# Moving a filter network's DMA issues from ScalarE's queue to SyncE's, and its steps closer together

## The chip, the cores and the metric

The kernel runs on one core of one Trainium2 chip. The metric is the device time of one execution in microseconds (us), from start to end of the program. It is one launch, with all layers inside.

## What is computed

The reference is a small hybrid network over 512 positions and 1024 features. It begins with two layers, each a mixer followed by a convolutional feed-forward block, and goes on with a second network of two layers (attention with a latent, then a Hyena mixer). Two pieces matter here. The first feed-forward block, `ffn(0)`:

```python
gate, val = jnp.split(x @ w_up, 2, axis=-1)        # 1024 -> 2 x 2816
conv = conv_b + sum(conv_w[j] * shifted(gate, j))  # width 3, along positions
y = (jax.nn.silu(conv) * val) @ w_down             # 2816 -> 1024
```

And two computations that don't depend on it, whose work is woven between its matmuls: the modulation rows of the later layers (`silu(c) @ ada_w`, called ada below), and the filters of the Hyena mixer. The latter come from a network over positions: three matmuls of 64 x 64, each followed by a sine (the hidden steps), then an output matmul whose rows are multiplied by a decay, folded into sums and differences, and kept in device memory until the Hyena mixer reads them.

## The kernel before

**Weights.** All weight matrices pass as one stream of chunks, each of 8 tiles of 128 x 128. SyncE loads a chunk (512 KB) into one of 4 `raw` buffers; ScalarE rounds it to a high half `whi` (L1195), VectorE subtracts to a low half `wlo` (L1871), with 3 buffers of each. TensorE does three matmuls a tile: high by high (L324), high by low (L327), low by high (L328). SyncE may load chunk c once the low half of chunk c - 4 is made; ScalarE may split chunk c once TensorE has begun chunk c - 2.

**`ffn(0)`** has two halves. Each half is an up pass of 11 rounds f (gate projection of 8 tiles, value projection of 8 tiles: two chunks a round), and a down pass of 8 projections i of 11 tiles. The first half takes chunks 40 to 72, the second 73 to 105. After each round VectorE and ScalarE run `tail(f)`: eviction of the gate (gp), convolution (c0, c1, c2), tanh, eviction of the value (v), products (s2, mo), high half (hh) and low half (hl) of the result. `tail` also contains two column products of ada (L2086, L2089), the first right behind gp and the second behind mo; behind that one is the filter's step.

**The filter's steps** are generators, one in each engine's program, advanced by `next(rows)`: once in each round f from 1 on, and in the down passes behind tile 9 of each projection and behind tile 4 of some. TensorE steps after a round's gate projection, ScalarE and VectorE in its `tail`. The generators must have the same number of steps. A unit n (four of them) has: wr (weights summed and subtracted, L2160), w_hi and w_lo (their halves, L1384, L2165), then eight steps ht (n, i, x) of two matmuls (L573, L574), which VectorE multiplies by the decay into `ab` (L2174). GpSimd (`folded`) adds and subtracts the two x of an i into `sd` (L2729).

**Their DMAs** are issued by ScalarE, in its own generator: the unit's weights (`weights`, L1353 and L1354), the decay (`decay`, L1359, for each x once at the unit's start and once for its second half), and the storing of `sd` to device memory (`keep`, L1364). Each issue waits in ScalarE's program order for its producer.

**SyncE's order** is written out by marks. TensorE's program, while it is built, notes at a place how many chunks it has begun, plus 3; SyncE issues the weights up to that chunk and then what the mark names. So far the marks in this block name the 24 ada rows of 512 KB (L2802, into 3 buffers), one for a round or projection, noted behind its last tile:

```python
def mark(self, name, more=0):
    self.s.marks[name] = -(-len(self.spec) // 8) + 3 + more
...
for name, at in sorted(s.marks.items(), key=lambda x: x[1]):
    weights(done, at)
    done = max(done, at)
```

Of the kernel before, what the change touches and what calls it, by code (L numbers as in the profile page):

```python
# [17 lines left out]
KD = 8  # L18
# [262 lines left out]
MLA_BANKS = [{"tr0": 7, "tr1": 4, "qn": 5, "kn": 7, "knc": 4, "sg": 5}, {"qn": 7, "kn": 4, "knc": 5, "sg": 7}]  # L281
MLA_OUT_BANKS = [7, 4, 5, 3, 0, 1, 2, 6]
ROWS_AT = [(5, 2), (5, 6), (6, 2), (6, 6), (7, 0)]
two_steps = lambda half, i: i % 2 or half == 0 and i > 3
UNITS = [(0, 0), (1, 0), (0, 1), (1, 1)]


# [27 lines left out]
def tensor_program(e, m, s):  # L315
# [230 lines left out]
    def filter_rows():  # L546


        a = m.ffn[0]
        for l in range(3):  # L550
            if l:
                q.wait_ge(*s.made_a.at("hdn", l - 1))
            else:
                q.wait_ge(*s.pos.at())
                q.wait_ge(*s.filt.at())
                q.wait_ge(*s.rb.at("n1"))
            src = a.fa[:, 1, :] if l else a.pos[:, :]
            e.matmul(B[7][0:64, :], a.fw[:, l, :], src, start=True, stop=True).then_inc(*s.filled.tick("hid", l))
            yield
            yield  # L560
        for n in range(4):
            yield
            yield
            for i in range(4):
                for x in range(2):
                    if x or i or n:
                        q.wait_ge(*s.taken_v.at("ht", *((n, i, 0) if x else (n, i - 1, 1) if i else (n - 1, 3, 1))))
                    else:
                        q.wait_ge(*s.made_v.at("fx", 2))
                    q.wait_ge(*s.made_v.at("w_lo", n, i % 2))  # L570
                    q.wait_ge(*s.made_v.at("hdl", 1))
                    cs = slice(256 * x + 128 * (i // 2), 256 * x + 128 * (i // 2) + 128)
                    e.matmul(B[7], a.hd[:, cs], a.ws[:, i % 2, :], start=True, stop=False)  # L573
                    e.matmul(B[7], a.hdl[:, cs], a.ws[:, i % 2, :], start=False,  # L574
                             stop=True).then_inc(*s.filled.tick("ht", n, i, x))
                    yield
        yield

    def ffn(layer):
# [34 lines left out]
        for half in range(2):  # L614
            for f in range(half * HF, half * HF + HF):
                run(project(2 * f % 6, up, f, ("gate", layer, f), nhi, nlo, bank_free(half, f, 0),
                            ready0 if f == 0 else nothing, then=behind(f, 0)))
                if f:
                    another()
                run(project((2 * f + 1) % 6, up, FT + f, ("val", layer, f), nhi, nlo, bank_free(half, f, 1),  # L620
                            then=behind(f, 1)))
                if f > 1:
                    next(ad, None)

            def ready(k, half=half):
                q.wait_ge(*s.hid_lo.at("f", layer, half * HF + k))

            for i in range(KD):
                f0 = half * HF + HF - 3

                def free(i=i, f0=f0):
                    if i >= 6:
                        q.wait_ge(*s.h.at(dn, half, i - 6))
                        return
                    for f in range(f0, f0 + 3):
                        for j in range(2):
                            if (2 * f + j) % 6 == i:
                                q.wait_ge(*s.taken_v.at("gv"[j], layer, f))
                run(project(i % 6, dn, i, (dn, half, i), hh, hl, free, ready, ks=HF, k0=half * HF,
                            then={4: another, 9: another} if two_steps(half, i) else {9: another}))  # L640
                if half == 0:
                    next(ad, None)

# [539 lines left out]
            yield  # L1183


def scalar_program(e, m, s, A, chunks):
    q = Waits(e)
    pc = Views(m).par
    B, PS, stat, par = m.bank, m.PS, m.stat, m.par
# [155 lines left out]

    def filter_rows():
        a = m.ffn[0]

        def weights(n):
            od, c = UNITS[n]  # L1350
            base = od * 2048 + 512 * c
            q.wait_ge(*(s.taken_v.at("ht", n - 1, 3, 1) if n else s.hid_lo.at("o", KD - 1)))
            e.dma_start(a.wd[64:128, 0, :], A["filt_out"][:, base:base + 512]).then_inc(*s.fo0.tick(n))  # L1353
            e.dma_start(a.wd[64:128, 1, :], A["filt_out"][:, base + 1024:base + 1536]).then_inc(*s.fo1.tick(n))  # L1354

        def decay(n, k, x):
            c = UNITS[n][1]
            q.wait_ge(*(s.taken_v.at("ht", n, 1, x) if k else s.made_v.at("w_lo", n, 1)))
            e.dma_start(a.wd[:, x, :], A["decay"][:, 2 * x + k, 512 * c:512 * c + 512]).then_inc(*s.dc[x].tick(n, k))  # L1359

        def keep(n, i):
            for x in range(2):
                q.wait_ge(*s.made_p.at("sd", n, i, x))
                e.dma_start(A["rows"][UNITS[n]][:, 4 * (i % 2) + 2 * x + i // 2, :],  # L1364
                            a.sd[:, x, :]).then_inc(*s.kept[x].tick(n, i))

        for l in range(3):
            q.wait_ge(*s.made_v.at("fa", l))
            e.activation(a.fa[:, 1, :], a.fa[:, 0, :], ACT.Sin).then_inc(*s.made_a.tick("hdn", l))
            if l == 2:  # L1370
                q.wait_ge(*s.made_a.at("hdn", 2))
                for x in range(2):
                    e.activation(a.hd[64 * x:64 * x + 64, :], a.fa[:, 1, :], ACT.Copy).then_inc(*s.made_a.tick("hd", x))
            yield
            if l == 1:
                weights(0)
            yield
        for n in range(4):
            if n:
                keep(n - 1, 3)  # L1380
            q.wait_ge(*(s.filled.at("ht", n - 1, 3, 1) if n else s.filled.at("hid", 2)))
            for j in range(2):
                q.wait_ge(*s.made_v.at("wr", n, j))
                e.activation(a.ws[0:64, j, :], a.wd[0:64, j, :], ACT.Copy).then_inc(*s.made_a.tick("w_hi", n, j))  # L1384
            yield
            for x in range(2):
                decay(n, 0, x)
            yield
            for i in range(4):
                for x in range(2):  # L1390
                    if i and x == 0:
                        keep(n, i - 1)
                    if i == 1:
                        decay(n, 1, x)
                    elif i == 3 and x and n < 3:
                        weights(n + 1)
                    yield
        keep(3, 3)
        yield

    def ffn(layer):
        a = m.ffn[layer]
# [21 lines left out]
        for half in range(2):  # L1424
# [19 lines left out]
            for i in range(KD):  # L1444
                for k in range(HF):
                    w.tiles(1)
                    if k == 9 or k == 4 and two_steps(half, i):
                        next(rows, None)
                if half and layer == 0:
                    after("n2", "attn_norm", i, (dn, 1), free=("val", 0, FT - 1))  # L1450
                elif half:
                    q.wait_ge(*s.h.at(dn, 1, i))
                    if i > 1:
                        q.wait_ge(*s.made_v.at("n4f", i - 1))
                        q.wait_ge(*s.acc.at("n4", i - 1))
                    e.activation(m.sqb[:, 1, :] if i else m.rb2[:, :], m.hT[:, i, :], ACT.Square,
                                 scale=m.fg[:, i:i + 1]).then_inc(*s.sq.tick("n4f", i))
                    e.activation(m.sqb[:, 0, :] if i else m.acc, m.hT[:, i, :], ACT.Square,
                                 scale=D ** -0.5).then_inc(*s.sq.tick("n4", i))
# [404 lines left out]
def vector_program(e, m, s, chunks):  # L1864
# [280 lines left out]
    def filter_rows():  # L2145
        a = m.ffn[0]
        for l in range(3):
            hidden(l)
            yield
            yield  # L2150
        for n in range(4):
            if n == 0:
                for x in range(2):
# [23 lines left out]
    def ffn(layer):  # L2177
# [37 lines left out]
        for half in range(2):  # L2215
# [14 lines left out]
            for i in range(KD):  # L2230
                for k in range(HF):
                    w.tiles(1)
                    if k == 9 or k == 4 and two_steps(half, i):
                        next(rows, None)
                if half == 0:
                    next(ad, None)
# [445 lines left out]
def pool_program(e, m, s):  # L2682
# [57 lines left out]
            folded(n, i)  # L2740
    for i in range(1, KD):
        sum_of_squares("n2", i)
        if i in (2, 3, 4, 6):
            folded(3, (2, 3, 4, 6).index(i))
    q.wait_ge(*s.filled.at("down0", 1, KD - 1))
    e.memset(m.swa.kz[:, :, :, :], 0.0).then_inc(*s.made_p.tick("kz"))
    e.memset(m.swa.vz[:, :, :, :, :], 0.0).then_inc(*s.made_p.tick("vz"))
# [33 lines left out]
def sync_program(e, m, s, A, chunks):  # L2781
# [11 lines left out]
    def ada_rows(layer, n):  # L2793
# [2 lines left out]
            q.wait_ge(*s.made_v.at("col", layer, 1 - layer, n - r))  # L2796
        elif layer == 0:
            q.wait_ge(*s.hid_lo.at("o", KD - 1))
        else:
            for x in range(2):  # L2800
                q.wait_ge(*s.kept[x].at(3, 3))
        e.dma_start(m.ffn[layer].aw[:, n % r, :], A["ada"][layer, n]).then_inc(*s.ada_w[n % r].tick(layer, n))  # L2802

    def filter_rows(od, c, j):
        if od or c:
# [17 lines left out]
    for name, at in sorted(s.marks.items(), key=lambda x: x[1]):  # L2823
# [13 lines left out]
            e.dma_start(m.ffn[0].fw[:, :, :], A["filt"]).then_inc(*s.filt.tick())  # L2837
        elif name[0] == "ada":
            ada_rows(*name[1:])
        else:  # L2840
            filter_rows(*name[1:])
    weights(done, NONE)
# [6 lines left out]
def build(nc, A, chunks, counted, notes):  # L2849
# [3 lines left out]
    with ExitStack() as ctx:  # L2853
# [24 lines left out]

        @block.scalar
        def _(e):  # L2880
            passed.append(scalar_program(e, m, s, A, chunks))

        @block.vector
        def _(e):
# [193 lines left out]
```

## Time and profile before

| | |
|---|---|
| median of 3 runs | 2054.27 us (2053.4 to 2057.48) |
| profiled execution, its own time | 2053.4 us |
| its span, first to last instruction | 2051.6 us |
| TensorE matmul busy | 1981.9 us, 97% |
| VectorE busy | 1381.3 us, 67% |
| ScalarE busy | 828.3 us, 40% |
| GpSimd busy | 231.9 us, 11% |
| mean granted TensorE clock | 0.987 of full speed |
| DMA | 208.4 MB, mean 102 GB/s |

PE is TensorE's matmul, PEld its weight load, DVE VectorE, ACT ScalarE, POOL GpSimd, SP SyncE; a q behind an engine is its sequencer, which waits and issues. L324 is line 324. The engines run at the same time, so busy shares don't add up to the span; what sets the time is which engine the others wait for at each place.

### The profile page before, as it was taken

Reading aid. Unit: us, or ns where it says so; the run is one execution under the profiler, and the core shown is the slowest. Engines: PE = TensorE matmul, PEld = TensorE weight load, DVE = VectorE, ACT = ScalarE, POOL = GpSimd, SP = SyncE. Lnnn points to the kernel's source line nnn. Section 1 sums busy time; section 2 is a strip of 40 time slices with the busy share of each in tenths; the row PEclk is TensorE's granted clock in tenths of the full one; section 3 lists DMA queues with packets and bytes.
Section 4 is the critical chain, followed back from the end, with each engine's and each line's share of the span. In section 5 each row is a group of like instructions: output and inputs, shape, how many; then the busy total and the mean of one; then the engine's idle time right before and its main releaser. Section 6 shows DMA issues by size and latency. Waiting matters only on the chain.

```text
span 2051.6 us, 24676 instructions
## 1 busy us (share of the span) xinstructions
PE 1981.9 (97%) x9878; PEld 1655.7 (81%) x9878; DVE 1381.3 (67%) x1961; ACT 828.3 (40%) x1259; POOL 231.9 (11%) x234
## 2 busy tenths in 40 slices
PE   8999999999999999999999999999999999999987
PEld 6888887778878888888888888778888878888776
DVE  5577765887789667756764784555555567787774
ACT  5333324442233345544432443444334444454442
POOL 2133221002201230010000001100000101001011
PEclk9999999999999999999999999999999999999998
DMA  5211113335534340123344333311111323232321
GB/s 190 63 64 53 52 56 99 124 133 180 192 138 163 123 144 32 42 62 140 140 161 134 125 132 103 103 62 42 42 42 32 115 81 117 96 137 91 126 83 51
DMA packets 60963, 208.40 MB, mean 102 GB/s; under 512 B 6832, under 2 KB 7152, under 8 KB 59696
## 3 DMA queue, kind: packets, MB, share of 16 engines
q1 hardware_dynamic: 53296, 193.19, 27.9%
q10 hardware_dynamic: 7552, 13.64, 1.9%
q8 instruction: 78, 1.28, 0.3%
q14 instruction: 37, 0.30, 0.0%
HBM read 196.31 MB, written 10.49 MB: 101 GB/s over the span
## 4 chain that ended last, share of the span: by engine, by line
PE 75%; DVE 16%; ACT 5%; issue 3%; DMA 0%; POOL 0%; ACTq 0%; SPq 0%; DVEq 0%
PE PS L324 19%; PE PS L328 19%; PE PS L327 19%; DVE wlo L1871 3%; PE PS L436 2%; PE PS L935 2%; DVE col_f L2086 2%; ACT whi L1195 1%; PE PS L331 1%; PE PS L334 1%; PE PS L335 1%; PE PS L924 1%; PE PS L687 1%; PE PS L386 1%; PE PS L728 1%
## 5 line engine op out<-in xcount | busy, mean ns | idle before, releaser
L324 PE MATMUL PS<-nhi,whi 128*128 128x512 f32 x1456 | 594.0, 408 | 20.9 <-DVE wlo L1871 5.9
L328 PE MATMUL PS<-nhi,wlo 128*128 128x512 f32 x1456 | 572.3, 393 | 0.0
L327 PE MATMUL PS<-nlo,whi 128*128 128x512 f32 x1456 | 571.1, 392 | 0.0
L1871 DVE TENSOR_TENSOR wlo<-raw,whi 128x1024 fp32r<-128x1024 f32 x291 | 368.7, 1276 | 183.0 <-ACT whi L1195 181.9
L1195 ACT ACTIVATE whi<-raw 128x1024 fp32r<-128x1024 f32 x291 | 303.1, 1052 | 211.7 <-PE PS L324 143.9
L324 PEld LDWEIGHTS PS<-nhi,whi 128*128 128x128 f32 x1456 | 276.4, 190 | 84.1 <-issue 11.3
L328 PEld LDWEIGHTS PS<-nhi,wlo 128*128 128x128 f32 x1456 | 275.6, 189 | 60.1
L327 PEld LDWEIGHTS PS<-nlo,whi 128*128 128x128 f32 x1456 | 276.8, 190 | 53.6 <-issue 2.6
L2713 POOL TENSOR_TENSOR diag<-diag,sqb 128x512 f32<-128x512 f32 (+1 forms) x56 | 73.1, 1305 | 783.9 <-ACT sqb L1204 701.3
L324 PE MATMUL PS<-hh_f,whi 128*128 128x512 f32 x352 | 137.2, 390 | 0.0
L328 PE MATMUL PS<-hh_f,wlo 128*128 128x512 f32 x352 | 137.0, 389 | 0.0
L327 PE MATMUL PS<-hl_f,whi 128*128 128x512 f32 x352 | 136.9, 389 | 0.0
L2729 POOL TENSOR_TENSOR sd_f<-ab_f 128x512 f32<-128x512 f32 x32 | 54.4, 1717 | 280.1 <-DVE ab_f L2174 279.5
L2086 DVE SCALAR_TENSOR_TENSOR col_f<-aw_f,scv,col_f 128x1024 f32<-128x1024 f32 x63 | 85.0, 1358 | 0.0
L328 PEld LDWEIGHTS PS<-hh_f,wlo 128*128 128x128 f32 x352 | 66.1, 188 | 13.8
L324 PEld LDWEIGHTS PS<-hh_f,whi 128*128 128x128 f32 x352 | 66.1, 188 | 13.7
L327 PEld LDWEIGHTS PS<-hl_f,whi 128*128 128x128 f32 x352 | 66.1, 188 | 13.7
L1413 ACT ACTIVATE t_f<-gp_f,par 128x512 f32<-128x512 f32 x44 | 35.9, 817 | 90.4 <-DVE gp_f L2191 90.4
L1659 ACT ACTIVATE pt_m<-PS 128x768 f32<-128x768 f32 x32 | 25.9, 811 | 111.8 <-PE PS L924 111.8
L1915 DVE TENSOR_TENSOR hT<-hT,PS 128x512 f32<-128x512 f32 x48 | 32.7, 682 | 52.2 <-PE PS L328 52.2
L436 PEld LDWEIGHTS PS<-qa,kk 128*128 128x128 f32 x448 | 56.0, 191 | 14.2 <-DVE qa L2023 10.3
L1204 ACT ACTIVATE sqb<-hT 128x512 f32<-128x512 f32 x42 | 26.5, 630 | 99.1 <-DVE hT L1915 62.4
(356 smaller groups left out, 3374.9 us busy)
## 6 DMA issues: line engine op xcount, KB each, us to landing
raw<-in_stream SPq DMA_DIRECT2D x291, 512.0 KB, 3.5
aw_f<-in_ada SPq DMA_DIRECT2D x48, 512.0 KB, 4.5
rows<-sd_f ACTq DMA_DIRECT2D x32, 256.0 KB, 2.2
rows_h<-rows SPq DMA_DIRECT2D x8, 1024.0 KB, 6.2
wd_f<-in_decay ACTq DMA_DIRECT2D x16, 256.0 KB, 3.0
hT<-in_xT SPq DMA_DIRECT2D x8, 256.0 KB, 6.8
out<-hT SPq DMA_DIRECT2D x8, 256.0 KB, 2.0
wd_f<-in_filt_out ACTq DMA_DIRECT2D x8, 128.0 KB, 2.8
```

Of the source, the lines that this page charges most:

```text
L324: op = e.matmul(out, hi, xh, start=first, stop=False)
L327: e.matmul(out, hi, xl, start=False, stop=False)
L328: return e.matmul(out, lo, xh, start=False, stop=last)
L436: op = e.matmul(B[b][:, cs], kk[:, z, cs], qx[:, cs], start=True, stop=True)
L935: op = e.matmul(B[6][:, 128 * blk:128 * blk + 128], a.v[:, t, 128 * h:128 * h + 128], a.pt[:, i, 128 * t:128 * t + 128], start=t == 0, sto ...
L1195: e.activation(m.whi[:, c % HL, :], m.raw[:, c % RAW, :], ACT.Copy).then_inc(*s.w_hi.tick(c))
L1413: e.activation(a.t[:, 0, z, :], a.gp[:, z, 2:T + 2], ACT.Identity, bias=pc(cb, f), scale=pc(cw, 44 + f)).then_inc(*s.made_a.tick("c0", lay ...
L1871: e.tensor_tensor(m.wlo[:, c % HL, :], m.raw[:, c % RAW, :], m.whi[:, c % HL, :].bitcast(F), SUB).then_inc(*s.w_lo.tick(c))
L1915: op = e.tensor_tensor(h, h, B[b], ADD)
L2086: e.scalar_tensor_tensor(col[:, v, :], aw[:, n % AW[layer], :], m.scv[:, 2, k, v:v + 1], col[:, v, :], MUL, ADD).then_inc(*s.made_v.tick(" ...
L2713: e.tensor_tensor(acc, acc, m.sqb[:, i % 2 if site != "n4" else 0, 0:width], ADD).then_inc(*s.acc.tick(site, i))
L2729: e.tensor_tensor(a.sd[:, x, :], a.ab[:, 0, :], a.ab[:, 1, :], SUB if x else ADD).then_inc(*s.made_p.tick("sd", n, i, x))
```

## The change

The DMA issues of the filter rows are taken out of ScalarE's generator. TensorE's generator notes marks for them, and SyncE issues them in the order of the marks, with the same waits. At equal places the mark noted first comes first.

The generators lose three steps: a hidden step is followed at once by the next (before, an empty step stood behind each). So the hidden steps stand at rounds 1, 2 and 3, where they stood at 1, 3 and 5, and every later step comes three steps earlier. The down pass of the first half has two steps for the odd projections only (before, also for 4 and 6). GpSimd's last four folds stand at other places among its sums of squares. And the first ada load of layer 1 no longer waits for the last stores.

```diff
-two_steps = lambda half, i: i % 2 or half == 0 and i > 3
...
@@ tensor_program, filter_rows
             else:
+                tiles.mark(("filter", 0))
                 q.wait_ge(*s.pos.at())
...
             e.matmul(B[7][0:64, :], a.fw[:, l, :], src, start=True, stop=True).then_inc(*s.filled.tick("hid", l))
             yield
-            yield
         for n in range(4):
-            yield
-            yield
+            if n:
+                tiles.mark(("kept", n - 1, 3))
+                tiles.mark(("filter", n))
+            yield
+            yield
+            for x in range(2):
+                tiles.mark(("decay", n, 0, x))
             for i in range(4):
                 for x in range(2):
+                    if i and x == 0:
+                        tiles.mark(("kept", n, i - 1))
+                    if (i, x) in ((1, 1), (2, 0)):
+                        tiles.mark(("decay", n, 1, 1 - x))
...
+        tiles.mark(("kept", 3, 3))
         yield
...
@@ tensor_program, ffn (the same in scalar_program and vector_program)
-                            then={4: another, 9: another} if two_steps(half, i) else {9: another}))
+                            then={4: another, 9: another} if i % 2 else {9: another}))
...
@@ scalar_program, filter_rows
-        def weights(n):
-        def decay(n, k, x):
-        def keep(n, i):
...
-            if l == 1:
-                weights(0)
-            yield
         for n in range(4):
-            if n:
-                keep(n - 1, 3)
...
-            yield
-            for x in range(2):
-                decay(n, 0, x)
-            yield
-            for i in range(4):
-                for x in range(2):
-                    if i and x == 0:
-                        keep(n, i - 1)
-                    if i == 1:
-                        decay(n, 1, x)
-                    elif i == 3 and x and n < 3:
-                        weights(n + 1)
-                    yield
-        keep(3, 3)
-        yield
+            for _ in range(10):
+                yield
...
@@ vector_program, filter_rows
         for l in range(3):
             hidden(l)
             yield
-            yield
...
@@ pool_program
-        if i in (2, 3, 4, 6):
-            folded(3, (2, 3, 4, 6).index(i))
+        if i in (1, 2, 4, 5):
+            folded(3, (1, 2, 4, 5).index(i))
...
@@ sync_program
-        else:
-            for x in range(2):
-                q.wait_ge(*s.kept[x].at(3, 3))
         e.dma_start(m.ffn[layer].aw[:, n % r, :], A["ada"][layer, n]).then_inc(*s.ada_w[n % r].tick(layer, n))
+
+    def filter_weights(n):
+        od, c = UNITS[n]
+        base = od * 2048 + 512 * c
+        wd = m.ffn[0].wd
+        q.wait_ge(*(s.taken_v.at("ht", n - 1, 3, 1) if n else s.hid_lo.at("o", KD - 1)))
+        e.dma_start(wd[64:128, 0, :], A["filt_out"][:, base:base + 512]).then_inc(*s.fo0.tick(n))
+        e.dma_start(wd[64:128, 1, :], A["filt_out"][:, base + 1024:base + 1536]).then_inc(*s.fo1.tick(n))
+
+    def decay(n, k, x):
+        c = UNITS[n][1]
+        q.wait_ge(*(s.taken_v.at("ht", n, 1, x) if k else s.made_v.at("w_lo", n, 1)))
+        e.dma_start(m.ffn[0].wd[:, x, :], A["decay"][:, 2 * x + k, 512 * c:512 * c + 512]).then_inc(*s.dc[x].tick(n, k))
+
+    def keep(n, i):
+        for x in range(2):
+            q.wait_ge(*s.made_p.at("sd", n, i, x))
+            e.dma_start(A["rows"][UNITS[n]][:, 4 * (i % 2) + 2 * x + i // 2, :],
+                        m.ffn[0].sd[:, x, :]).then_inc(*s.kept[x].tick(n, i))
...
+        elif name[0] == "filter":
+            filter_weights(*name[1:])
+        elif name[0] == "decay":
+            decay(*name[1:])
+        elif name[0] == "kept":
+            keep(*name[1:])
```

## Rows read from the trace of the kernel before

**Rows 1.** The page: the chain that ended last, by engine.

```profile
PE 75%; DVE 16%; ACT 5%; issue 3%; DMA 0%; POOL 0%; ACTq 0%; SPq 0%; DVEq 0%
```

**Rows 2.** Windows of the passes: busy PE, PEld, DVE, ACT, POOL; granted clock, DMA share, GB/s.

```profile
345.00:475.00 130.00, 123.99 (x536) 98.28 (x536) 109.66 (x142) 57.42 (x70) 0.00 (x0) 0.99 0.39 133
475.00:542.00 67.00, 66.33 (x296) 54.68 (x296) 51.64 (x50) 12.98 (x14) 23.86 (x16) 1.00 0.56 199
542.00:665.00 123.00, 121.05 (x537) 99.71 (x535) 101.37 (x118) 41.44 (x51) 15.16 (x10) 0.97 0.44 153
665.00:760.00 95.00, 95.00 (x428) 78.67 (x428) 59.70 (x72) 37.21 (x51) 32.98 (x23) 0.98 0.40 128
```

**Rows 3.** Waits of TensorE, 350 to 760 us: total us, times, longest us.

```profile
PE PS L324 <- DVE wlo L1871: 3.2, 2, 2.8
PE PS L573 <- DVE ws_f L2165: 3.0, 2, 2.1
PE PS L573 <- DVE ab_f L2174: 2.3, 4, 0.7
```

**Rows 4.** Timeline of TensorE: start, us, line, tiles [idle before <-releaser].

```profile
355.11 1.07 PE L558 MATMUL PS<-pos,fw 64*64 64x512 f32 x2
...
361.70 0.39 PE L324 MATMUL PS<-nhi,whi 128*128 128x512 f32 x1
...
367.14 0.39 PE L324 MATMUL PS<-nhi,whi 128*128 128x512 f32 x1
...
402.24 1.07 PE L558 MATMUL PS<-fa,fw 64*64 64x512 f32 x2
...
422.65 0.80 PE L324 MATMUL PS<-nhi,whi 128*128 128x512 f32 x1 [2.78 <-DVE wlo L1871]
...
453.77 0.47 PE L573 MATMUL PS<-ws_f,hd_f 128*128 128x512 f32 x1 [2.07 <-DVE ws_f L2165]
...
454.31 0.40 PE L324 MATMUL PS<-nhi,whi 128*128 128x512 f32 x1
```

**Rows 5.** Timeline of VectorE, first up pass.

```profile
423.65 0.68 DVE L2191 TENSOR_TENSOR gp_f<-PS,rb 128x512 f32<-128x512 f32 x1
...
433.07 0.68 DVE L2191 TENSOR_TENSOR gp_f<-PS,rb 128x512 f32<-128x512 f32 x1
...
439.63 1.40 DVE L2155 TENSOR_TENSOR hdl_f<-fa,hd_f 64x512 fp32r<-64x512 f32 x2
441.06 1.29 DVE L2160 TENSOR_TENSOR wd_f<-wd_f 64x512 f32<-64x512 f32 x2
...
459.37 1.27 DVE L2086 SCALAR_TENSOR_TENSOR col_f<-aw_f,scv,col_f 128x1024 f32<-128x1024 f32 x1
```

**Rows 6.** Waits of all engines, 450 to 755 us.

```profile
ACT whi L1195 <- DVE ab_f L2174: 25.0, 5, 10.3
...
ACT whi L1195 <- POOL sd_f L2729: 20.4, 3, 10.3
```

**Rows 7.** Timelines of VectorE and ScalarE, hidden step 0.

```profile
365.87 0.80 DVE L2126 TENSOR_SCALAR fa<-PS,par 64x512 f32<-64x512 f32 x1
...
369.95 0.63 ACT L1369 ACTIVATE fa<-fa 64x512 f32<-64x512 f32 x1 [2.04 <-DVE fa L2142]
```

**Rows 8.** Tiles sd_f, rows and aw_f: durations in ns and us to landing, min/median/max.

```profile
L2729 POOL TENSOR_TENSOR sd_f<-ab_f x32: 1279/1591/2287, 475.2 to 744.2; 128x512 f32<-128x512 f32 x32
...
L1364 ACTq DMA_DIRECT2D rows<-sd_f x32: 321/332/445, 476.6 to 745.6; - x32
...
DMA to landing us min/median/max: 4.2/4.5/6.7
```

**Rows 9.** Timeline of SyncE's queue.

```profile
445.25 0.33 SPq L2788 DMA_DIRECT2D raw<-in_stream  x1
445.62 0.43 SPq L2802 DMA_DIRECT2D aw_f<-in_ada  x1
```

**Rows 10.** Tile hh_f: first and last start of the down-projection's matmuls.

```profile
L324 PE MATMUL PS<-hh_f,whi x352: 389/389/486, 475.6 to 1295.9; 128*128 128x512 f32 x176
```

More of the change, by code:

```diff
@@ L1183, in steps, with scalar_program @@
             yield
-def scalar_program(e, m, s, A, chunks):
+def scalar_program(e, m, s, chunks):
     q = Waits(e)
@@ L1347, in filter_rows @@
         a = m.ffn[0]
-        def weights(n):
[L1350 to L1354, printed above, removed]
-        def decay(n, k, x):
-            c = UNITS[n][1]
-            q.wait_ge(*(s.taken_v.at("ht", n, 1, x) if k else s.made_v.at("w_lo", n, 1)))
-            e.dma_start(a.wd[:, x, :], A["decay"][:, 2 * x + k, 512 * c:512 * c + 512]).then_inc(*s.dc[x].tick(n, k))
-        def keep(n, i):
-            for x in range(2):
-                q.wait_ge(*s.made_p.at("sd", n, i, x))
-                e.dma_start(A["rows"][UNITS[n]][:, 4 * (i % 2) + 2 * x + i // 2, :],
-                            a.sd[:, x, :]).then_inc(*s.kept[x].tick(n, i))
         for l in range(3):
@@ L1446, in ffn @@
                     w.tiles(1)
-                    if k == 9 or k == 4 and two_steps(half, i):
+                    if k == 9 or k == 4 and i % 2:
                         next(rows, None)
@@ L2232, in ffn @@
                     w.tiles(1)
-                    if k == 9 or k == 4 and two_steps(half, i):
+                    if k == 9 or k == 4 and i % 2:
                         next(rows, None)
@@ L2798, in ada_rows @@
             q.wait_ge(*s.hid_lo.at("o", KD - 1))
-        else:
-            for x in range(2):
-                q.wait_ge(*s.kept[x].at(3, 3))
         e.dma_start(m.ffn[layer].aw[:, n % r, :], A["ada"][layer, n]).then_inc(*s.ada_w[n % r].tick(layer, n))
+    def filter_weights(n):
[14 more added lines that the diff above has]
+                        m.ffn[0].sd[:, x, :]).then_inc(*s.kept[x].tick(n, i))
     def filter_rows(od, c, j):
@@ L2880, in _ @@
         def _(e):
-            passed.append(scalar_program(e, m, s, A, chunks))
+            passed.append(scalar_program(e, m, s, chunks))
         @block.vector
```

## The prediction, made before the change was run

> **What bounds the kernel now.** The reading starts with the chain of work that ended last: three quarters of it is TensorE [rows 1], so only what makes TensorE wait, repeat work or run slow can move the time. The change touches only the first feed-forward block, which lies between 345 and 760 us, so the windows come next [rows 2]. They cut that stretch into its four passes: first up-projection, first down-projection, second up, second down. TensorE is idle for 6.0, 0.7, 1.95 and 0 us in them, 8.6 us of 415. The waits view names whom it waited for [rows 3]: 8.5 us in all, always VectorE, either for the low half of a weight chunk or for the filter rows. The granted clock of the first, third and fourth windows is 0.99, 0.97 and 0.98, which is 1.3, 3.7 and 1.9 us lost at the lower level (1.2 instead of 2.4 GHz).
>
> The block's own beat is read from two starts. A chunk of 8 weight tiles (24 matmuls) takes 367.14 - 361.70 = 5.44 us [rows 4]. One round f of an up pass is two chunks, 10.9 us on TensorE, and a filter-row matmul pair adds 0.54 us (454.31 - 453.77). VectorE's round, from one gate eviction to the next, is 433.07 - 423.65 = 9.4 us without any filter work [rows 5]; a filter step adds 0.7 (an ht product, as gp), 1.3 (w_lo, two operations like wr) or 2.7 us (hdl 1.40 and wr 1.29). So in the up passes VectorE has about 1 us a round to spare. That is the number on which this case turns: whatever delays VectorE there is handed to TensorE nearly in full.
>
> **The change, part by part.**
>
> *Issues leave ScalarE.* 56 DMA issues (32 kept, 16 decay, 8 filter weights) of 0.32 to 0.6 us each [rows 8] are some 20 us of ScalarE's queue. ScalarE also waited for their producers ahead of weight splits, 25.0 + 20.4 us [rows 6]. But TensorE's waits of rows 3 amount to 8.5 us and most come from VectorE's own load, so I price this at nothing. If that cover were wrong the most it can give is the 8.5 us.
>
> *The hidden steps move together.* The three small matmuls of the filter network stand at rounds 1, 3 and 5 (355.11 the first, 402.24 the third) [rows 4]; now at 1, 2, 3. Each needs the sine of the previous, made at the end of VectorE's round. Sine 0 ends at 369.95 + 0.63 = 370.6 [rows 7]; TensorE reaches the second matmul at 367.14: it waits 3.4 us. Then value projection 2 ends 6.5 us later at 377.1; VectorE needs v, s2, mo (2.1), one column product (0.75) and the seven hidden operations (from 365.87 to the sine's start at 369.95, 4.1) and ScalarE the sine: 384.9. TensorE is ready at 382.5 and waits 2.4 us. The third hidden step and the wr step now follow each other without an idle round between them. Adding VectorE's operations round by round: low half for the chunk of round 5 at 403.5 against 402.3, 1.2 us; the next one, behind wr, 417.2 against 414.5, 2.7 us; w_lo of unit 0 at 425.9 against 422.7, 3.2 us. Sum 12.9 us where the before has 6.0: **+6.9 us**.
>
> *The issues join SyncE's queue.* This is the big term. SyncE issues in program order and waits in it. A mark stands three chunks ahead of TensorE. The weight load ahead of it waits only for a split far back: at 445.25 SyncE issues a chunk that TensorE first reads at 475.6 [rows 10], 30 us later, and right behind it, at 445.62, the modulation rows (ada) [rows 9], which VectorE uses at 459.37 [rows 5]. That is 13.7 us from issue to use; they land in 4.2 to 6.7 us [rows 8], so 7 to 9.5 us are to spare. After the change a kept issue stands before such a pair of loads, and waits for GpSimd's sum of the filter step at the end of VectorE's current round. Call that step's end T. GpSimd needs 2 x 1.28 to 2 x 2.29 us [rows 8]: release at T + 2.6 to 4.6, two kept issues and one chunk later the ada rows are issued at T + 4 to 5.4 and land at T + 9 to 10. VectorE wants them at T + 3.8 (hl 0.69, two low halves 2.36, gp 0.68) up to T + 6 where GpSimd slows it. VectorE stands about 4.7 us, in mid-round, with c1, c2, mo and the next low halves behind it, and TensorE behind those. Where the wait is for the filter step itself (decay 1) it is about 2.8 us, where for w_lo (decay 0) 3.7.
>
> Placing each mark by its tile count: first up pass, rounds 6, 8, 9 (3.7 + 4.7 + 2.8 = 11.2, less some 3 of VectorE's slack): **+8**. Second up pass, rounds 12, 14, 16, 17, 18 (4.7 + 3.7 + 4.7 + 2.8 + 4.7 = 20.6), plus the w_lo wait that is there now, less 5 of slack: 17, against 2: **+15**. First down pass: there are ada loads too, marked at the end of a projection and used at the same place, so they are late at i = 1, 2, 3, 5, 6, 7; but VectorE is idle 15 of 67 us there [rows 2]. Following i = 2 to 4, w_lo of unit 1 comes 2.6 us late and a low half 1.9 us: 4.5 against 0.7, **+4**. Second down pass: no ada rows, and weight chunks have 10 us and more in hand: 0. Sum 6.9 + 8 + 15 + 4 = **+34 us**. TensorE's own work is the same; two small matmuls only move.
>
> The removed wait of layer 1's first ada load for the stores, long landed by then, is worth nothing. The 3 fewer steps and GpSimd's earlier places among the squares fall in a pass in which TensorE never waits.
>
> The row on which this rests shows SyncE with nothing between loads, so a rule on queues has to be weighed. The Trainium skill ("DMA: Bandwidth & Descriptors", Issuing engines are not separate DMA queues) says all issuers feed the same 16 DMA engines and spreading issues saves only the sequencer's issue time. By that rule alone the move costs 20 us of an idle SyncE, nothing in the sum, and the change would stand at +7; no row here shows it, as ScalarE and SyncE issues never stood in one queue. The same page (the chain of events of a DMA) has the semaphore waits on the issuing sequencer, which is what my term needs.
>
> **Base.** The profiled execution took 2053.4 us (span 2051.6), 0.9 below the median 2054.3 of the runs. 2053.4 + 34 = 2087.4; I give 2087.
>
> **Rivals.**
> 1. *Only the compression counts.* Ada loads land in time, because the marks fall early enough or VectorE is itself late. For it: 7 to 9.5 us of spare. Against: the hold lasts from a low half until the end of the next round, 12 us. 2053.4 + 7 = 2060. This is also what the skill's rule above gives. Chance 0.13.
> 2. *Faster.* ScalarE's splits are what makes VectorE late: the 2.8 us wait for a low half [rows 3, 4] comes as ScalarE stands in its filter steps. Freed of issues and waits, the splits come early and up to 8.5 us of waits go, with the low-clock stretch after the longest: 2053.4 - 8.5 - 1.3 = 2044. It decides if SyncE's holds stay under the 7 us to spare, and if the sine is no longer waited for; but the sine wait follows from two rows. Chance 0.07.
> 3. *Worse than the sum.* DMAs bunch behind each hold (two stores, two chunks, ada rows), so ada rows land as late as the 6.7 us of the slowest and some weight chunks too: ten late loads by 2 us more is +20: 2107. Chance 0.14.
> 4. *Nothing to see*, gains and losses cancel: 2054. Chance 0.04.
>
> The forecast, 0.62, has its own range 2074 to 2101: stalls of 3.7 instead of 4.7 us at the lower end; at the upper, slack that GpSimd's slowing has eaten, and low-clock stretches. Those follow stretches in which TensorE idles (clock 0.99 in the window with the 2.8 us wait), at 1.3 to 3.7 us a window; I count as many as before. With rival 1 inside and rival 3 mostly inside, 2059 to 2108. A difference under 0.2% (4 us) can't be told from none: faster 0.07, same 0.04, slower 0.89.
>
> **What would show it.** Right: TensorE waiting for the sine of ScalarE near 367 and 382 us; VectorE's column products (L2086, L2089) idle before them, released by a DMA, in rounds 6, 8, 9, 12, 14, 16 to 18; SyncE's own waits naming GpSimd's sums and VectorE's filter steps; most of the loss between 540 and 700 us and nothing after 770. Wrong: column products without idle time (rival 1), or ScalarE's splits earlier and waits for low halves gone (rival 2). The prediction fails in size if SyncE's release comes much earlier than T + 4, or if VectorE has more in hand than 1 us a round.

## The result and the profile after

The changed kernel takes 2102.6 us (median of 4, 2101.2 to 2102.9) where the runs of before have 2055.9 (median of 4, 2053.4 to 2058.5): ratio 1.0226, 95% interval 1.0208 to 1.0244, 2.3% slower. The spans of the profiled executions differ by about the same amount, 2098.6 - 2051.6 = 47.0 us. The prediction was 2087 in a range of 2059 to 2108.

The page after: the chain by engine, and the group of VectorE's column products (line 2058 is line 2086 of before). The chain's shares add up to 65%: it is followed back from the end only to 745 us, so it says next to nothing of the block that was changed, and the windows and waits below have to.

```profile
PE 55%; DVE 6%; ACT 3%; issue 1%; POOL 0%; DVEq 0%; ACTq 0%
...
L2058 DVE SCALAR_TENSOR_TENSOR col_f<-aw_f,scv,col_f 128x1024 f32<-128x1024 f32 x63 | 83.2, 1329 | 44.7 <-DMA aw_f<-in_ada 44.7
```

The group has 44.7 us of idle time in front of it, and what ended it is the DMA of the modulation rows. In before, the group never waited:

```profile
L2086 DVE SCALAR_TENSOR_TENSOR col_f<-aw_f,scv,col_f 128x1024 f32<-128x1024 f32 x63 | 85.0, 1358 | 0.0
```

Windows over the four passes and the rest, cut at the same chunks in both, first after, then before: busy PE, PEld, DVE, ACT, POOL; granted clock, DMA share, GB/s.

```profile
336.70:496.60 159.90, 141.00 (x587) 111.60 (x586) 120.45 (x154) 60.87 (x75) 9.21 (x8) 0.94 0.33 115
496.60:568.50 71.90, 68.00 (x286) 54.67 (x287) 45.96 (x45) 12.73 (x13) 15.47 (x11) 0.97 0.48 164
568.50:728.40 159.90, 144.12 (x611) 117.95 (x610) 110.50 (x131) 44.97 (x55) 16.82 (x12) 0.91 0.37 133
728.40:795.00 66.60, 64.01 (x282) 52.43 (x281) 41.73 (x43) 21.73 (x29) 24.11 (x18) 1.00 0.42 140
795.00:2098.60 1303.60, 1257.74 (x6373) 1058.36 (x6371) 849.21 (x1263) 564.11 (x919) 73.25 (x58) 0.99 0.27 93
```

```profile
336.40:475.60 139.20, 132.98 (x582) 105.69 (x580) 115.94 (x151) 60.51 (x75) 1.86 (x3) 0.99 0.39 132
475.60:542.00 66.40, 65.73 (x290) 54.08 (x291) 51.13 (x49) 12.75 (x13) 23.51 (x16) 1.00 0.56 200
542.00:680.80 138.80, 136.85 (x611) 113.07 (x610) 110.93 (x131) 45.24 (x55) 18.13 (x12) 0.96 0.41 143
680.80:744.70 63.90, 63.90 (x283) 52.93 (x282) 39.20 (x44) 21.84 (x29) 23.96 (x18) 1.00 0.46 147
744.70:2051.60 1306.90, 1261.77 (x6373) 1061.72 (x6371) 848.75 (x1263) 563.94 (x919) 74.14 (x59) 0.99 0.27 92
```

The passes are 20.7, 5.5, 21.1 and 2.7 us longer (+50.0), and the rest, whose work is the same, 3.3 shorter. TensorE's idle time in the passes (length less busy) is 18.9, 3.9, 15.8 and 2.6 us, against 6.2, 0.7, 1.95 and 0: +32.3. The other 17.7 us of the 50 are busy time: the same matmuls take longer, and the granted clock is 0.94 and 0.91 in the up passes where before has 0.99 and 0.96. Over the whole execution TensorE's idle time grows by 33.2 us and its busy time, for the same 9878 matmuls, by 1995.7 - 1981.9 = 13.8. Together they are the 47.0. The granted clock of the whole gives nearly the same for the second part: 2098.6 x (1 - 0.981) = 39.9 us against 2051.6 x (1 - 0.987) = 26.7, +13.2.

Waits of TensorE over the block, 345 to 810 us, in answer to [rows 3]: total, times, longest.

```profile
PE PS L581 <- DVE ab_f L2145: 23.2, 7, 5.1
PE PS L581 <- DVE ws_f L2136: 7.2, 4, 2.8
PE PS L323 <- DVE wlo L1843: 5.3, 4, 2.0
PE PS L558 <- ACT fa L1359: 5.3, 2, 3.3
```

41.0 us instead of 8.5. The sine (L558) is new; ab_f is the wait for VectorE's product of a filter step, ten times what it was.

Where they stand, by TensorE's timeline, in answer to [rows 4]:

```profile
370.92 1.24 PE L558 MATMUL PS<-fa,fw 64*64 64x512 f32 x2 [3.33 <-ACT fa L1359]
...
386.62 1.07 PE L558 MATMUL PS<-fa,fw 64*64 64x512 f32 x2 [1.95 <-ACT fa L1359]
...
442.72 0.50 PE L581 MATMUL PS<-ws_f,hd_f 128*128 128x512 f32 x1 [3.97 <-DVE ab_f L2145]
...
472.43 0.79 PE L581 MATMUL PS<-ws_f,hd_f 128*128 128x512 f32 x1 [5.14 <-DVE ab_f L2145]
...
745.45 0.47 PE L581 MATMUL PS<-ws_f,hd_f 128*128 128x512 f32 x1 [2.59 <-DVE ws_f L2136]
```

First come the two sine waits; behind them TensorE waits for two low halves (1.21 us at 405.45 and 1.99 at 418.65) and for w_lo of unit 0 (1.12 us). Then come waits of 3 to 5 us for VectorE. There are five of these: 3.97, 5.14, 3.26, 4.32 and 5.07 us. The longest wait of before is 2.78.

One of these, that of 472.43, is taken apart. VectorE's timeline (the filter product of round 7, the gate of round 8, its column product, its filter product):

```profile
453.68 0.68 DVE L2145 TENSOR_TENSOR ab_f<-PS,wd_f 128x512 f32<-128x512 f32 x1
...
459.35 0.68 DVE L2162 TENSOR_TENSOR gp_f<-PS,rb 128x512 f32<-128x512 f32 x1
465.73 1.28 DVE L2058 SCALAR_TENSOR_TENSOR col_f<-aw_f,scv,col_f 128x1024 f32<-128x1024 f32 x1 [5.70 <-DMA aw_f<-in_ada]
...
471.69 0.68 DVE L2145 TENSOR_TENSOR ab_f<-PS,wd_f 128x512 f32<-128x512 f32 x1
```

GpSimd's second sum of that filter step, and SyncE's queue (a line's second number is the time to the end of the last of its issues):

```profile
456.77 1.58 POOL L2700 TENSOR_TENSOR sd_f<-ab_f 128x512 f32<-128x512 f32 x1
```

```profile
431.32 0.74 SPq L2759 DMA_DIRECT2D raw<-in_stream  x1
456.14 2.57 SPq L2788 DMA_DIRECT2D rows<-sd_f  x2
458.75 0.44 SPq L2759 DMA_DIRECT2D raw<-in_stream  x1
459.23 2.07 SPq L2770 DMA_DIRECT2D aw_f<-in_ada  x1
```

The filter step ends at T = 453.68 + 0.68 = 454.4. SyncE had its weights out by 432 and stood in the wait for the first sum until 456.14, then in that for the second; GpSimd ends at 456.77 + 1.58 = 458.35, T + 4.0. The chunk goes out at 458.75, the modulation rows at 459.23, T + 4.9. VectorE is ready at 459.35 + 0.68 = 460.0, T + 5.7, and gets them at 465.7, T + 11.4: 5.70 us idle. Its next filter product is at 471.69, and TensorE, ready at 467.3, starts at 472.43. In before the same rows, behind the same chunk, had been issued 14.5 us before their use at 446.88:

```profile
432.42 0.43 SPq L2802 DMA_DIRECT2D aw_f<-in_ada  x1
```

Two of the other column products that waited in the up passes:

```profile
436.02 1.28 DVE L2058 SCALAR_TENSOR_TENSOR col_f<-aw_f,scv,col_f 128x1024 f32<-128x1024 f32 x1 [4.81 <-DMA aw_f<-in_ada]
...
683.58 1.28 DVE L2058 SCALAR_TENSOR_TENSOR col_f<-aw_f,scv,col_f 128x1024 f32<-128x1024 f32 x1 [5.12 <-DMA aw_f<-in_ada]
```

They are rounds 6 and 18; rounds 9, 12, 14, 16 and 17 waited too (the table below has all). Six more, of 1.1 to 5.1 us and 17.8 in sum, are in the first down pass. There TensorE's idle time grows by only 3.2 us.

SyncE's own waits for stores and decays, new in this queue, and the landing times of the modulation rows [rows 8]:

```profile
SPq L2788 <- POOL sd_f L2700: 230.3, 32, 24.1
...
SPq L2783 <- DVE ws_f L2136: 59.3, 4, 20.8
```

```profile
DMA to landing us min/median/max: 4.1/4.9/8.9
```

The median landing, over all 48 loads of modulation rows in the program, went from 4.5 to 4.9 us and the slowest from 6.7 to 8.9. The loads now leave in bunches behind each hold. Late landing by itself is not what costs, though: in e7 below the slowest takes 10.9 us, and no column product waits.

### The profile page after: what moved, and what is told of

It is laid out like the page before. It is cut to its first block, busy times and chain, and to the rows that moved or that the text cites. A ratio compares the mean times of both kernels' runs of the same rounds, so it can differ in the third digit from the quotient of the medians.

```text
span 2098.6 us, 24674 instructions
## 1 busy us (share of the span) xinstructions
PE 1995.7 (95%) x9878; PEld 1663.3 (79%) x9878; DVE 1383.4 (66%) x1961; ACT 828.4 (39%) x1259; POOL 229.3 (11%) x234
## 4 chain that ended last, share of the span: by engine, by line
PE 55%; DVE 6%; ACT 3%; issue 1%; POOL 0%; DVEq 0%; ACTq 0%
PE PS L323 15%; PE PS L327 15%; PE PS L326 15%; PE PS L944 2%; PE PS L933 1%; PE PS L696 1%; PE PS L737 1%; DVE wlo L1843 1%; PE PS L330 1%; PE PS L334 1%; PE PS L333 1%; ACT s_s L1454 1%; ACT whi L1204 1%; PE PS L718 0%; PE PS L385 0%
## 5 line engine op out<-in xcount | busy, mean ns | idle before, releaser
L323 PEld LDWEIGHTS PS<-nhi,whi 128*128 128x128 f32 x1456 | 279.1, 192 | 86.8 <-issue 11.5
L2058 DVE SCALAR_TENSOR_TENSOR col_f<-aw_f,scv,col_f 128x1024 f32<-128x1024 f32 x63 | 83.2, 1329 | 44.7 <-DMA aw_f<-in_ada 44.7
L326 PEld LDWEIGHTS PS<-hl_f,whi 128*128 128x128 f32 x352 | 66.7, 189 | 13.8
L1388 ACT ACTIVATE t_f<-t_f 128x512 f32<-128x512 f32 x44 | 27.8, 632 | 100.6 <-DVE t_f L2169 100.6
```

The costliest lines, as they stand in the source:

```text
L323: op = e.matmul(out, hi, xh, start=first, stop=False)
L326: e.matmul(out, hi, xl, start=False, stop=False)
L1388: e.activation(a.t[:, 2, z, :], a.t[:, 1, z, :], ACT.Tanh, scale=0.5).then_inc(*s.made_a.tick("th", layer, f))
L2058: e.scalar_tensor_tensor(col[:, v, :], aw[:, n % AW[layer], :], m.scv[:, 2, k, v:v + 1], col[:, v, :], MUL, ADD).then_inc(*s.made_v.tick(" ...
```

## The experiments

All were timed beside the kernel before on the same chip. Ratios are to those runs.

**e1_steps_only: the packed steps alone.** From the kernel before: the second `yield` behind a hidden step goes in all three engines, `two_steps` becomes `i % 2`, GpSimd's folds move as in the change; ScalarE keeps all issues.

```diff
             e.matmul(...).then_inc(*s.filled.tick("hid", l))
             yield
-            yield
```

> Only the steps move together (rounds 1, 2, 3); all filter DMAs stay with ScalarE. Theory (late modulation rows behind SyncE's holds make most of the loss): VectorE's column products wait for no DMA, TensorE waits for the sine twice (3.5 and 2.1 us) and for the low halves and w_lo behind them, 12 to 14 us in the first up pass instead of 6; the device time is 6 to 8 us above before, plus 2 to 5 us of low clock: 2062 to 2069. Rival (the packed steps make most of the loss, the queue costs only issue time): 2090 to 2100.

Measured: 2061.9 us, ratio 1.0022 (1.0011 to 1.0033). TensorE's waits:

```profile
PE PS L558 <- ACT fa L1368: 5.3, 2, 3.3
PE PS L324 <- DVE wlo L1869: 4.0, 3, 2.0
```

No column product waits for a DMA. The waits are the 5.3 us for the sine, as expected, 4.0 for low halves, 1.2 for w_lo (the prediction had 3.2) and 1.2 for ab_f: 11.7 us in the block, 10.3 of them in the first up pass, where 12 to 14 were expected. The time is just under the 2062 to 2069 that were expected. The rival falls.

**e2_queue_only: the queue alone.** From the changed kernel, with the old step spacing put back.

> Only the issues move to SyncE's queue, marks as in the change; the steps stand as before (hidden steps at rounds 1, 3, 5). Theory: column products wait 35 to 50 us for modulation rows, TensorE 25 to 33 us in the block, and the low-clock stretches multiply: 2085 to 2098. Rival (moving issues between queues saves or costs only issue time): 2053 to 2058.

Measured: 2088.0 us, ratio 1.0154 (1.0136 to 1.0171). TensorE's waits, and VectorE's for modulation rows:

```profile
PE PS L583 <- DVE ab_f L2149: 18.2, 6, 5.0
PE PS L324 <- DVE wlo L1846: 8.3, 5, 3.2
```

```profile
DVE col_f L2061 <- DMA aw_f<-in_ada: 38.5, 10, 5.4
```

With 2.8 us for w_lo TensorE waits 29.3 us. Most of the loss is here, without any packing. The two parts alone make 0.22 + 1.54 = 1.8% of the 2.3%; together they make more than their sum. Why was not tried.

**e7_ada_first: the direct test.** The changed kernel with one number altered. The stores, decays and weights of the filter keep their places in the queue; the modulation rows go in front of them.

```diff
-                tiles.mark(("ada", layer, KD * g + k))
+                tiles.mark(("ada", layer, KD * g + k), 0 if layer else -2)
```

> The change as it is, with all filter marks in their places; only the marks of layer 0's modulation rows stand two chunks earlier, so that SyncE issues the rows of a round ahead of the filter's wait. Theory (the late modulation rows are what the holds cost): column products wait for DMA under 8 us instead of 49, SyncE still waits about as long for GpSimd's sums, and the time falls to that of the packed steps alone, 2060 to 2070. Rival (the holds cost through late weight chunks or through the stores, not through the modulation rows): 2090 to 2103.

Measured: 2062.0 us, ratio 1.0035 (1.0023 to 1.0048). TensorE's waits, VectorE's only wait for a DMA, and SyncE's:

```profile
PE PS L558 <- ACT fa L1359: 5.3, 2, 3.3
PE PS L581 <- DVE ws_f L2136: 4.0, 2, 2.9
PE PS L323 <- DVE wlo L1843: 3.2, 2, 2.0
```

```profile
DVE wd_f L2131 <- DMA wd_f<-in_filt_out: 5.8, 2, 3.7
```

```profile
SPq L2788 <- POOL sd_f L2700: 202.2, 32, 18.8
...
SPq L2783 <- DVE ws_f L2136: 55.4, 4, 20.7
```

SyncE still stands 202 us in waits for GpSimd (230 before the edit) and 55 in those for w_lo (59). It costs nothing that can be measured now, because what is queued behind the waits is not needed soon. 49 us of waiting column products are gone, and about 40 of the 47 us with them. What is left, 1.0035, can't be told from the 1.0022 of the packed steps alone. This shows the cause: the late modulation rows. It is not the holding up of the queue by itself, nor late weight chunks, nor DMA bandwidth: SyncE still waits nearly as long, the chunks keep their places behind the holds, and the bytes are the same.

**e6_only_kept_late: which holds.** The changed kernel, the marks of the stores two chunks later.

```diff
-                        tiles.mark(("kept", n, i - 1))
+                        tiles.mark(("kept", n, i - 1), 2)
```

> The change as it is, but the marks of the stores (kept) two chunks later; the decay and filter marks stay. Theory, by the waits in the trace of the change: the TensorE waits of 5.3, 4.5 and 5.2 us behind stores go, those behind decays (4.1 and 3.4 us) stay, and some low-clock stretches go with the former: 2077 to 2085. Rival (all holds are alike to the queue, the last to release decides): above 2095.

Measured: 2075.0 us, ratio 1.0092 (1.0075 to 1.0109).

```profile
PE PS L581 <- DVE ab_f L2145: 10.3, 7, 3.7
```

```profile
DVE col_f L2058 <- DMA aw_f<-in_ada: 20.4, 7, 4.7
```

That is two microseconds under what was expected. 20.4 us of the column products' 49 stay, most of them behind decays and weights, and 10.3 of TensorE's 23.2. The change loses 40.6 us against e7, and 27.6 of them go here: the stores' holds make about two thirds of the queue's cost. The profiled execution was the fastest of the six, 2068.4 us at a granted clock of 0.988, so its rows are for the waits only.

**e3_late_marks: all marks two chunks later.** The same edit for the stores, decays and weights.

> The change as it is, but every filter mark behind the first stands two chunks later in SyncE's order, so that the modulation rows of the round are issued ahead of the wait. Theory: waits of column products for DMA fall from 49 us to under 8, and the time to that of the packed steps alone, 2060 to 2069. Rival (SyncE's queue or the DMA engines are too full, whatever the order): stays at 2095 to 2103.

Measured: 2076.6 us, ratio 1.0095 (1.0081 to 1.0109), 8 us above what was expected. No column product waits, as expected, but something else is late:

```profile
PE PS L581 <- DVE ws_f L2136: 13.6, 3, 6.1
```

```profile
DVE wd_f L2131 <- DMA wd_f<-in_filt_out: 13.8, 2, 6.9
```

The next unit's weights now leave so late that VectorE waits 6.9 us for them twice, and TensorE 4.7 and 6.1 us for the w_lo made from them (the third wait of the 13.6 us is unit 0's, 2.8). The queue has two sides: too early and it holds the modulation rows, too late and its own cargo is late.

**e4_late_marks_old_steps** is the same with the old spacing.

> Marks two chunks later and the steps spaced as before: ScalarE is free of the 56 issues and their waits at no cost to the modulation rows. Theory: within 4 us of before, 2050 to 2058, as TensorE's waits come from VectorE's own load. Rival (ScalarE's issues and waits are what makes the splits late): 2042 to 2048.

Measured: 2060.6 us, ratio 1.0021 (1.0009 to 1.0032), with the same late weights (10.3 us of VectorE's). It is 3 us above what was expected, in part at least for that reason: TensorE waits 4.3 us for w_lo behind them.

**e8_ada_first_old_steps and e5_marks_tuned: is there something to win?** Both have the old spacing and all issues on SyncE, and mark the next unit's weights one step earlier; e8 puts modulation rows first, e5 puts the filter's marks two chunks later.

The lines that e5 changes in e4:

```diff
-                tiles.mark(("filter", n), 2)
...
+                    if n < 3 and (i, x) == (3, 1):
+                        tiles.mark(("filter", n + 1), 2)
```

> SyncE's queue as in the change, modulation rows two chunks earlier, steps spaced as before, and the weights of the next unit marked one step earlier, where ScalarE issued them. Theory: both costs are gone, so the time is before's within its noise, 2051 to 2059. Rival (the queue has a cost of its own): 2065 or more.

> As the kernel with marks two chunks later and old steps, and the next unit's weights marked one step earlier. Theory: the 10 us that VectorE waited for those weights, and the 4.3 us of TensorE's behind them, go: 2051 to 2057. If ScalarE's release from its issues is worth anything it shows here as a time under before's 2053 to 2056.

Measured: 2058.6 us, ratio 1.0015 (1.0006 to 1.0025), for e8, and 2057.7, ratio 1.0013 (1.0003 to 1.0022), for e5, which is just above its range. TensorE's waits in e5:

```profile
PE PS L584 <- DVE ws_f L2141: 4.8, 2, 2.7
PE PS L324 <- DVE wlo L1847: 2.5, 2, 2.1
PE PS L584 <- DVE ab_f L2150: 1.4, 1, 1.4
```

8.7 us, as in before. ScalarE is rid of 56 issues and its waits for GpSimd, and nothing is won. No version tried beats the kernel before. The traces say why for its longest wait, the low half at round 5: VectorE waits the same 2.50 us for ScalarE's split in before, e5 and e8, and ahead of the split ScalarE stands in the hidden step, where it waits 3.2 us for VectorE's operations and then makes the sine and two copies. No DMA issue is among them.

**e9_hidden_packed: the sine alone.** The kernel before with the hidden steps at rounds 1, 2, 3 and three empty steps behind them, so that every later step stands where it did.

> The kernel before with the three hidden steps at rounds 1, 2, 3 and three empty steps behind them, so that every later step stands where it did and ScalarE issues all DMAs. If the sine's latency and the bunching of VectorE's work are what the packed steps cost: TensorE waits 3.5 and 2.1 us for the sine and 1 to 2 us for a low half, but not again at rounds 4 and 5, and the later waits of before (2.1 us for w_lo) stay or shrink; some 2 to 5 us above before, 2056 to 2060. Rival (the cost comes from the units' steps standing three earlier): the time of before, under 2056.

Measured: 2058.4 us, ratio 1.0015 (1.0006 to 1.0024).

```profile
PE PS L558 <- ACT fa L1370: 5.3, 2, 3.3
...
PE PS L324 <- DVE wlo L1873: 1.4, 1, 1.4
```

The sine waits are the same 5.3 us; in exchange the 2.8 us wait for a low half at 422.65 has gone, and one of 1.4 has come at 405.95. TensorE waits 11.5 us in the block, 3.0 more than in before, where e1 has 3.2 more. This is within the expectation and differs little from e1: most of what the packing costs is in the hidden steps. The units' earlier start adds 0.07% by the two ratios, which their intervals don't separate from none.

## Why the prediction was right, and what was mis-sized

| term | predicted | measured |
|---|---|---|
| sine waits | 3.4 + 2.4 | 3.33 + 1.95 |
| low halves, rounds 5 and 6 | 1.2 + 2.7 | 1.21 + 1.99 |
| w_lo of unit 0 | 3.2 | 1.12 |
| packed steps, sum less before | 12.9 - 6.0 = +6.9 | 9.6 - 6.2 = +3.4 |
| modulation rows late, VectorE, rounds 6, 8, 9 | 3.7 + 4.7 + 2.8 = 11.2 | 4.81 + 5.70 + 0.66 = 11.2 |
| the same, rounds 12, 14, 16, 17, 18 | 4.7 + 3.7 + 4.7 + 2.8 + 4.7 = 20.6 | 4.20 + 4.11 + 4.87 + 1.73 + 5.12 = 20.0 |
| TensorE idle, first up pass | +15 | +12.7 |
| first down pass | +4 | +3.2 |
| second up pass | +15 | +13.8 |
| second down pass | 0 | +2.6 |
| longer matmuls (low clock), whole program | 0 | +13.8 |

**The queue.** The place of each hold, counted by tiles, was right for all eight rounds and all six projections. The release at T + 2.6 to 4.6 came at T + 4.0 in the event taken apart; landing at T + 9 to 10 was early by 1.4 us there: five DMAs leave within 5.2 us, and the issue of the modulation rows alone takes 2.07 us where the median is 0.43. The singles differ by up to 2 us, the sums hardly. e7 shows that this is the cause and e2 its size by itself.

**The beat.** VectorE's one spare microsecond a round was the number on which the sum turned. TensorE's waits of 5.14 and 5.07 us behind column products that waited 5.70 and 5.12 show that nearly all of a long delay is handed on. Of the shorter ones less is: in sum TensorE's five waits are 21.8 us behind 31.2 of the column products'.

**The packed steps.** The two sine waits follow from a timeline's rows to within half a microsecond. (The second was added up wrong: its own terms give 384.7 and a wait of 2.2 us, not 384.9 and 2.4.) The sum of +6.9 was twice what was measured, and most of that is w_lo. TensorE came to it at 426.0 and not at 422.7, as it had been through two low-clock stretches by then (granted clock 0.67 in 370 to 375 and 0.66 in 418 to 423 us, together 3.4 us); w_lo itself was only 1.2 us later than I had added up.

**ScalarE's issues** at nothing: right, by e8 and e5, in which nothing is won.

**The second down pass** was put at 0 because no modulation rows are there. But unit 3's weights are there: marked together with a store, they wait for it and go out at 734.99; VectorE waits 3.42 us for them, and TensorE 2.59 for w_lo at 745.45. One of the signs did not come as said either: most of the loss was to lie between 540 and 700 us, but the first up pass, before 500, has 20.7 us of it and the second 21.1.

**The clock** is the term that was mis-sized. The idle time came out as summed, +33.2 us against +34; the matmuls' 13.8 us longer busy time was put at nothing. Together they are the 13 us between 2087.4 and the profiled execution's 2100.4; the median of the runs lies 2.2 us above that execution. That the idle time came out is luck in part: the packed steps were 3.5 us less than put, the second down pass and the queue in the first up pass more. I wrote that low-clock stretches follow stretches in which TensorE idles, and then counted "as many as before", while adding 34 us of idle time in pieces of 3 to 5 us. A row of before had what was needed: the matmul behind the 2.78 us wait at 422.65 takes 0.80 and not 0.39 us [rows 4].

**The rivals.** Rival 1 (only the compression counts, 2060) is what e1 and e7 measure, when the queue is taken out. Rival 2 (faster) falls by e5. Rival 3 (2107) had the right remark, bunched loads land later (8.9 us at the slowest). One weight chunk was late too: ScalarE waits 7.76 us for it until 577.80, but TensorE's next wait is near 607 us and 0.36 us long. The time came near rival 3's value through the clock, which is not its mechanism. By the rule of the Trainium skill ("DMA: Bandwidth & Descriptors", Issuing engines are not separate DMA queues), that issuing on several engines saves only the sequencer's issue time, the move would have been free. It costs nothing that the runs can separate in e7 and 1.5% in e2: the measurement decides. The same page of the Trainium skill (Anatomy of one DMA), in its account of a DMA issued by GpSimd, says that any semaphore wait happens on the issuing sequencer. The SyncE rows here agree: 230.3 us of its queue's waits are for GpSimd's sums.

## What to carry to other kernels

Moving a DMA's issue to another queue moves its wait too. Before it is moved, ask what is queued behind the place, when that has to be issued to land in time, and when the wait ends; a queue that runs ahead of the consumers (here by 30 us for a weight chunk [rows 9, 10]) reaches the wait long before its producer is done. Order the loads that are needed soonest in front of waits for late producers: one number, two chunks, was worth 40 us here. And where a change adds idle pieces of several microseconds to TensorE, add the slower clock that follows them.

## What the runs showed of the hardware

Each of the five waits of 3 to 5 us has a stretch at the lower clock behind it: the granted clock is 0.66 in 443 to 448, 0.54 in 472 to 478, 0.66 in 630 to 635, and 0.50 in 659 to 664 and 690 to 695 us. Over the whole program 33.2 us more of idle time came with 13.8 us more of busy time, 0.4 us for each.

It is no fixed price, and the length of a wait alone does not set it. Behind the 1.95 us at 386.62 the clock stays at 2.4 GHz (1.00 in 387 to 390), and behind the 2.76 us wait at 615.84 the matmuls take 0.39 to 0.40 us at once. But behind the 1.99 us at 418.65 they go to 0.63 us, 0.8 us after TensorE has started again:

```profile
418.00:423.00 5.00, 4.35 (x12) 3.44 (x13) 4.96 (x7) 1.10 (x2) 0.00 (x0) 0.66 0.00 0
...
472.00:478.00 6.00, 5.57 (x14) 4.43 (x15) 3.93 (x5) 1.84 (x3) 0.00 (x0) 0.54 0.73 263
```

e1 and e7, with 11.7 and 12.5 us of waits in the block, have before's mean clock of 0.987. The executions of one kernel differ in it too: the six of e6 have 0.983 to 0.988, and 2079.4 to 2068.4 us.

The rest of the program, the same work, took 3.3 us less in the changed kernel. Its matmuls are 4.0 us shorter there (1257.74 against 1261.77 us), and 1347 to 1647 us has a granted clock of 1.00 where the same stretch of before, 1300 to 1600, has 0.98. What moved that low-clock stretch was not tried.
